# RWKV-7 and attention block on one core: another start of the chunk stage, and VectorE's last lane operations at another place in its steps

## The reference

```
def step(S, inp):
    r_t, w_t, k_t, v_t, a_t, b_t = inp
    sa = jnp.einsum('bhij,bhj->bhi', S, a_t)
    S = (S * w_t[:, :, None, :] + sa[..., None] * b_t[:, :, None, :]
         + v_t[..., None] * k_t[:, :, None, :])
    return S, jnp.einsum('bhij,bhj->bhi', S, r_t)
...
seq_in = tuple(u.transpose(1, 0, 2, 3) for u in (r_h, w_h, k_h, v_h, -kk, kk * a_h))
_, y = lax.scan(step, S0, seq_in)
```

## Time and profile before

| | us |
|---|---|
| median of three runs (1510.53 to 1513.07) | 1511.58 |
| the profiled execution's own time | 1514.68 |
| its span, first to last instruction | 1513.0 |
| PE busy in it | 1436.7 (95%) |
| DVE busy | 1033.1 (68%) |
| ACT busy | 739.6 (49%) |
| chunk stage: its first `l_products` to its last `quads` | 878.15 to 1060.35 |

### The profile page before, as it was taken

One profiled execution on the slowest core, in us unless ns is written; L12 is line 12 of the kernel. 1 busy time (PEld: TensorE's weight loads), 2 busy tenths in 40 slices (PEclk: granted clock), 3 DMA queues, 4 the chain that ended last, 5 costly groups with the idle time before them and its releaser, 6 DMA issues.

```text
span 1513.0 us, 30344 instructions
## 1 busy us (share of the span) xinstructions
PE 1436.7 (95%) x12931; PEld 1322.3 (87%) x12931; DVE 1033.1 (68%) x1463; ACT 739.6 (49%) x1071; POOL 93.5 (6%) x120
## 2 busy tenths in 40 slices
PE   6999999999999999998999967999799999999997
PEld 5898898999999999998999756889467898899986
DVE  5667577588844787577868665776678884488732
ACT  4555465445532455457588532433454553255422
POOL 3010011000030000000000231110000000000010
PEclk9999999999999999999999977999999999999999
DMA  4212221423433333555222232332333343334331
GB/s 126 67 57 63 64 70 50 113 84 98 123 92 100 92 92 88 158 162 173 83 74 77 70 85 47 60 57 40 113 84 98 98 123 104 95 85 112 86 96 56
DMA packets 283990, 136.78 MB, mean 90 GB/s; under 512 B 65449, under 2 KB 278593, under 8 KB 283601
## 3 DMA queue, kind: packets, MB, share of 16 engines
q1 hardware_dynamic: 283552, 134.77, 32.4%
q10 hardware_dynamic: 304, 0.08, 0.0%
HBM read 124.33 MB, written 10.49 MB: 89 GB/s over the span
## 4 chain that ended last, share of the span: by engine, by line
PE 74%; DVE 11%; ACT 6%; issue 3%; DMA 3%; POOL 1%; SPq 0%; DVEq 0%; POOLq 0%; ACTq 0%
PE psg L1882 25%; PE psx L1723 13%; PE psg L1723 11%; PE psg L2688 6%; PE psg L590 2%; DVE w_lo L136 2%; PE psx L590 2%; PE psg L618 2%; PE psg L674 1%; ACT rest_hi L330 1%; PE psx L3334 1%; DVE rest_lo L429 1%; DVE sum_lo L446 1%; ACT rest L316 1%; ACT w_hi L132 1%
## 5 line engine op out<-in xcount | busy, mean ns | idle before, releaser
L132 ACT ACTIVATE w_hi<-w_raw 128x1024 fp32r<-128x1024 f32 (+1 forms) x122 | 141.9, 1164 | 209.8 <-PE psg L1882 148.1
L1882 PE MATMUL psg<-mid_hi_l,w_hi 128*128 128x264 f32 (+1 forms) x720 | 232.8, 323 | 2.3 <-DVE w_lo L136 1.3
L1882 PE MATMUL psg<-mid_lo_l,w_hi 128*128 128x264 f32 (+1 forms) x720 | 231.6, 322 | 0.0
L1882 PE MATMUL psg<-mid_hi_l,w_lo 128*128 128x264 f32 (+1 forms) x720 | 231.0, 321 | 0.0
L136 DVE TENSOR_TENSOR w_lo<-w_raw,w_hi 128x1024 fp32r<-128x1024 f32 (+1 forms) x121 | 165.0, 1365 | 77.5 <-ACT w_hi L132 77.0
L1882 PEld LDWEIGHTS psg<-mid_hi_l,w_hi 128*128 128x128 f32 x720 | 135.3, 188 | 14.1 <-DVE w_lo L136 2.0
L1882 PEld LDWEIGHTS psg<-mid_lo_l,w_hi 128*128 128x128 f32 x720 | 135.3, 188 | 10.5 <-issue 0.2
L1882 PEld LDWEIGHTS psg<-mid_hi_l,w_lo 128*128 128x128 f32 x720 | 135.4, 188 | 10.3
L2688 PE MATMUL psg<-x_hi,w_hi 128*128 128x264 f32 (+1 forms) x320 | 99.7, 312 | 7.9 <-DVE w_lo L136 7.9
L2688 PE MATMUL psg<-x_lo,w_hi 128*128 128x264 f32 (+1 forms) x320 | 98.8, 309 | 0.0
L2688 PE MATMUL psg<-x_hi,w_lo 128*128 128x264 f32 (+1 forms) x320 | 98.7, 309 | 0.0
(11 more groups left out here) (518 smaller groups left out, 4336.1 us busy)
## 6 DMA issues: line engine op xcount, KB each, us to landing
w_raw<-in_w_ffn_out_dram SPq DMA_DIRECT2D x40, 704.0 KB, 4.7
w_raw<-in_w_qkv_dram SPq DMA_DIRECT2D x24, 512.0 KB, 3.7
w_raw<-in_w_rkv_dram SPq DMA_DIRECT2D x24, 512.0 KB, 3.9
x_raw_l<-in_w_ffn_in_dram SPq DMA_DIRECT2D x18, 512.0 KB, 4.1
x_raw_l<-in_w_ffn_in_dram SPq DMA_DIRECT2D x36, 256.0 KB, 4.7
w_raw<-in_w_ffn_in_dram SPq DMA_DIRECT2D x16, 512.0 KB, 3.8
y_raw_l<-in_w_ffn_in_dram SPq DMA_DIRECT2D x16, 512.0 KB, 4.0
y_raw_l<-in_w_ffn_in_dram SPq DMA_DIRECT2D x32, 256.0 KB, 4.5
```

The source lines that it names most:

```text
L132: k.nc.scalar.activation(k.w_hi[j][:, 0:kt, :], k.raw[j][:, 0:kt, :], ACT.Copy).then_inc(k.hi_ready[j].h, 1)
L1882: done = k.nc.tensor.matmul(self.bank(i, c), w[:, t, :], x, start=t == 0 and n == 0, stop=t == count - 1 and n == 2)
```

## The change

It replaces the loop's three short first steps by a start written out for each engine, and changes the steps themselves in three places.

- **Start.** The loop begins at c = 0. Ahead of it PE, ACT, DVE, POOL and SP have their own sequences for chunks 0 to 2, with `keep(8)`, `keep(44)`, `keep(36)` and, in step 0, another `keep(8)`. SP issues the first store of `low` ahead of the zero fills. `l_products(2)` now stands behind chunk 0's `a_v`, and DVE's `products(2)` behind `last_blocks(1)`; `l_products(3)`, `products(3)` and `small_blocks(2)` are in step 0.
- **Two buffers.** `lane_x`, `lane_xt` and the DRAM buffer of `low` are doubled, so that `small_blocks(n)` waits for the stores of chunk n - 2 and not of chunk n - 1.
- **Steps.** In steps 1 to 6 DVE's `last_blocks(c + 2)` moves from behind `next_t` to a place between the first and the second half of the masks. In every step that prepares, `turn_v` becomes eight transposes in place of eight matmuls with the identity. The halves of partitions for values and solve are swapped, as are the two planes of `bk`.

```diff
...
+    kept = lambda name: nc.dram_tensor(name, [H, (C // W) * LANE], F32).ap()
+    k.low_kept = [kept(f"low_kept{q}") for q in range(2)]
...
-            sp.wait_ge(zero_r.h, 4)
+            keep_low(0)
+            sp.wait_ge(zero_r.h, 1)
...
-            for c in range(-3, CHUNKS - 2):
-                if c + 3 < CHUNKS:
-                    keep_low(c + 3)
-                    fetch_lanes(c + 3)
-                if c == -3:
...
-                    sp.wait_ge(inv_in.h, 64)
-                else:
-                    keep_inverse(c + 2)
-                    fetch_inverse(c + 2)
+            fetch_lanes(0)
+            keep_low(1)
+            fetch_lanes(1)
+            sp.wait_ge(scaled_v.h, 1)
...
+            sp.wait_ge(inv_in.h, 64)
+            for n in range(CHUNKS):
+                if 1 < n < CHUNKS - 1:
+                    keep_low(n + 1)
+                    fetch_lanes(n + 1)
+                keep_inverse(n)
+                fetch_inverse(n)
+                if n == 1:
+                    keep_low(2)
+                    fetch_lanes(2)
...
             decays(1)
+            lower(0)
+            keys_turned(0, 0)
+            decays(2)
+            lower(1)
+            values_turned(0, 0)
+            end_decay(0, 0)
+            av_out(0, 0)
+            act.wait_ge(g_in.h, (1 + P // G_REST) * 16)
+            nc.scalar.activation(r.g_hi[:], r.g_raw[:], ACT.Copy).then_inc(g_split.h, 1)
+            lower(2)
+            decays(3)
             steps(act, step)
...
-                else:
-                    dve.wait_ge(inv_out.h, 32 * n)
+                elif n > 1:
+                    dve.wait_ge(inv_out.h, 32 * (n - 1))
...
-                if prep and n:
+                if prep:
                     next_t(n)
-                if 0 <= c + 2 < CHUNKS:
-                    last_blocks(c + 2)
-                if prep and n:
+                if c == 0:
                     next_xt(n, p, 0)
                     next_xs(n, p)
...
+                    small_blocks(2)
+                if c == 0 or not prep and c + 2 < CHUNKS:
+                    last_blocks(c + 2)
+                if prep and c:
+                    next_xt(n, p, 0)
+                    next_xs(n, p)
+                if prep and c:
+                    grow(q, c)
                 if prep:
                     keys(n, 0)
                     reads(n, p, 0)
+                    if 0 < c < CHUNKS - 2:
+                        last_blocks(c + 2)
                     keys(n, 1)
                     reads(n, p, 1)
...
             products(1)
-            dve.wait_ge(scaled_v.h, 2)
+            small_blocks(0)
+            last_blocks(0)
+            keys(0, 0)
+            keys(0, 1)
+            small_blocks(1)
+            last_blocks(1)
+            products(2)
             steps(dve, step)
...
-                    last = mm(pair_ps[C:P, m // 4, (m % 4) * P:(m % 4) * P + P], r.vv[:, m, n * C:n * C + C], k.ident[:],
-                              start=True, stop=True)
+                    last = nc.tensor.transpose(pair_ps[0:C, m // 4, (m % 4) * P:(m % 4) * P + P],
+                                               r.vv[:, m, n * C:n * C + C], k.ident[:])
...
             front_evicted(pe)
+            l_products(0)
+            turn_bk(0)
+            keep(8)
+            l_products(1)
+            turn_v(0)
+            quads(0, 0)
+            keep(44)
+            quads(0, 1)
+            a_v(0, 0)
+            keep(36)
+            l_products(2)
             steps(pe, step)
```

More of the change, by code:

```diff
@@ L111, in setup @@
     k.res_kept = nc.dram_tensor("res_kept", [P, KT, T], F32).ap()
[L112 to L113 removed]
+    kept = lambda name: nc.dram_tensor(name, [H, (C // W) * LANE], F32).ap()
+    k.low_kept = [kept(f"low_kept{q}") for q in range(2)]
+    k.inv_kept, k.turned_kept = kept("inverse_kept"), kept("inverse_turned_kept")
     return k
@@ L2967, in steps @@
         def steps(eng, step):
-            for c in range(-3, CHUNKS):
-                step(c, c + 1, c % 2, 0 <= c, 0 <= c + 1 < CHUNKS)
+            for c in range(CHUNKS):
+                step(c, c + 1, c % 2, c + 1 < CHUNKS)
         res_in, g_in, g_split, gate_d, gate_r = (
@@ L3046, in decays, with lower @@
                 if n > 1:
-                    nc.scalar.activation(bk[(n - 1) % 3][:, :, 1, :], chunk(r.kk_in, n - 1), ACT.Copy).then_inc(bk_r.h, 1)
+                    nc.scalar.activation(bk[(n - 1) % 3][:, :, 0, :], chunk(r.kk_in, n - 1), ACT.Copy).then_inc(bk_r.h, 1)
                 nc.scalar.activation(ch.w_ext[:, :, 1:C + 1], chunk(r.gs, n), ACT.Exp, scale=DECAY)
                 nc.scalar.activation(ch.w_inv[:], chunk(r.gs, n), ACT.Exp, scale=-DECAY).then_inc(exps.h, 1)
-            def step(c, n, q, chain, prep):
+            def lower(n):
+                act.wait_ge(lps.h, n + 1)
+                nc.scalar.activation(low[n % 3][:], l_ps, ACT.Copy).then_inc(low_r.h, 1)
@@ L3052, in step @@
+            def step(c, n, q, prep):
                 p = 1 - q
-                if c + 3 < CHUNKS:
-                    act.wait_ge(lps.h, c + 4)
-                    nc.scalar.activation(low[c % 3][:], l_ps, ACT.Copy).then_inc(low_r.h, 1)
+                if c + 3 < CHUNKS and c:
+                    lower(c + 3)
                 if prep:
[L3057 to L3060, removed]
@@ L3078, in step @@
                         act.wait_ge(state_r.h, c)
[L3079 to L3082, removed]
-                    nc.scalar.activation(r.g_hi[:], r.g_raw[:], ACT.Copy).then_inc(g_split.h, 1)
-                if chain and not prep:
+                    end_decay(n, p)
+                if not prep:
                     act.wait_ge(dx_d.h, level_count(c, 1))
@@ L3308, in l_products @@
                 for h, m, rows in heads:
-                    last = mm(l_ps[rows, m, :], r.xn[rows, m, n * C:n * C + C], bk[n % 3][rows, m, 0, :],
+                    last = mm(l_ps[rows, m, :], r.xn[rows, m, n * C:n * C + C], bk[n % 3][rows, m, 1, :],
                               start=True, stop=True)
@@ L3357, in a_v @@
                 for h, m, rows in heads:
-                    last = mm(a_ps[rows, m, :], akm[C:P, at(h), :], uv[p][C:P, at(h), :], start=True, stop=True)
+                    last = mm(a_ps[rows, m, :], akm[0:C, at(h), :], uv[p][0:C, at(h), :], start=True, stop=True)
                 last.then_inc(av_d.h, 1)
@@ L3420, in chain_u @@
                 for h, m, rows in heads:
-                    last = mm(u_ps[0:C, h % 2, m * C:m * C + C], xt[q][rows, m, :], wt[rows, m, :], start=True,
+                    last = mm(u_ps[C:P, h % 2, m * C:m * C + C], xt[q][rows, m, :], wt[rows, m, :], start=True,
                               stop=True)
@@ L3450, in gate, with step @@
                    skip_group_check=True).then_inc(gate_d.h, 1)
-            def step(c, n, q, chain, prep):
+            def step(c, n, q, prep):
                 p = 1 - q
-                if c + 3 < CHUNKS:
-                    l_products(c + 3)
-                if c < -1:
-                    keep(24)
-                if prep:
+                if c == 0:
                     turn_bk(n)
-                if c == 0:
                     turn_v(n)
@@ L3464, in step @@
                     quads(n, 0)
+                    l_products(3)
+                    keep(8)
                     times_x(n, p, 0)
```

190 lines of the change are left out of this document (102 added, 88 removed).

## The result

The changed kernel takes **1544.57 us** (median of 4 runs, 1541.02 to 1547.45) against 1511.58 for the kernel before (median of three): a ratio of **1.0218, 95% interval 1.0188 to 1.0248**, so it is slower. A fourth execution of the kernel before took 2803.71 us and is in neither the median nor the ratio. The forecast was 1542.7 in 1521 to 1560. Its profiled execution took 1547.45, with a span of 1545.7 against 1513.0: +32.7. X(1) comes at 944.91 instead of 946.20 (-1.29), the six intervals to X(7) last 135.97 instead of 103.05 (+32.92), and what is behind X(7) 464.82 instead of 463.75 (+1.07). The loss is all in the six intervals, as forecast. Inside them it is not put together as forecast.

A forecast was written before the change was run, and what follows sets the result against it. The prediction saw idle time in the start, little in the steps, and the moved last_blocks' DRAM round trip setting six intervals. Start -4.5, round trip +27.7, step 7 -0.9, clock +8.8: +31.1 on 1511.58, so 1542.7, range 1521 to 1560.

The forecast's parts named there:

- last_blocks moved, through DRAM: Steps 1 to 6: the inverse, born later, reaches the next times_x later; 21.8 us per interval, +27.7 in all.
- So it sets all six intervals: X(1) to X(7), each step's first times_x: the 21.8 us round trip exceeds 19.7 and 17.1, giving 130.8 in all.
- wrong if `times_x` starts without waiting for a transfer: Sign in the steps that would refute the forecast: times_x not held by the inverse's transfer.
- The masks: Steps 1 to 6: last_blocks delays the second mask by 2.6; full steps 19.7 us, steps 5 and 6 about 17.1.
- The clock: Steps 1 to 6: new TensorE gaps lower its clock, 2.2 in four of six steps; +8.8, between 0 and 32.
- falling after 3 us with 0.6 idle in them: Trace reading behind the clock term: TensorE's clock fell after 3 us that held 0.6 idle.
- The start: Ahead of X(1), step 1's first times_x: the new order brings it earlier; -4.5, the middle of 0.3 and 8.7.
- the two ends -0.3 and -8.7: Start: X(1) 0.3 earlier at mostly half clock, 8.7 earlier at full clock.
- The nearer of the two sums: Start, sum with half clock: quads at 935.7 and X(1) at 945.9, 0.3 earlier.
- turn_v: Steps 1 to 7: eight transposes for 16 matmul instructions take 0.87 us off the path.
- Behind X(7): Step 7, after its first times_x: no last_blocks, and the transposes save 0.87; -0.9.
- The interval of 19.7 by the 2.0 us of "DMA: Bandwidth & Descriptors": Round trip with the skill's 2.0 us transfer cost: interval 19.7 instead of 21.8, six costing 15.1 instead of 27.7.

The follow-up runs named there:

- e1: Changed kernel with last_blocks put back ahead of the subtractions in steps 1 to 6, all else as changed: 1502.76 us, ratio 0.9940.
- e2: Changed kernel whose fetches from the third chunk on read the second chunk's stored inverse, so no round trip: 1528.10 us, ratio 1.0109.
- e11: e1 with SyncE's store of the inverse held until the step's second mask: 1543.38 us, ratio 1.0220.
- e8: e2 with 20 unused matmuls where TensorE waits for the second mask: 1520.33 us, ratio 1.0069.
- e4: Changed kernel with 20 unused matmuls where TensorE waits for the second mask, round trip kept: 1546.45 us, ratio 1.0229.
- e10: Changed kernel with last_blocks back in front in steps 1 to 4, behind the first masks in 5 and 6: 1518.35 us, ratio 1.0044.
- e6: e1 with SyncE's store of the inverse held until the copy of a_v: 1557.62 us, ratio 1.0295.
- e9: Changed kernel with last_blocks back in front in steps 5 and 6 only: 1524.68 us, ratio 1.0087.
- e5: e1 with turn_v's eight transposes written as matmuls with the identity: 1511.09 us, ratio 0.9981.
- e3: Changed kernel with GpSimd's products held until the first masks are done, round trip kept: 1546.95 us, ratio 1.0219.

## Why the prediction was right, and where it wasn't

Two bounds could set a step, and each was run alone, at the clock that it left TensorE. Sums of intervals in us:

| | four full steps | last two |
|---|---|---|
| before | 71.77 | 31.28 |
| e1, neither | 67.31 | 29.20 |
| chain through the mask alone (e2) | 88.24 | 33.82 |
| round trip alone (e11) | 89.88 | 46.41 |
| both (the changed kernel) | 90.11 | 45.86 |

- **last_blocks moved, through DRAM: right in mechanism, 0.9 small.** Forecast 21.8 an interval; e11 shows 22.7 in the mean, and 21.70 in its one interval at full clock. The forecast had 12.6 from X to the store and 9.2 from there to X. The second is right (9.19 in the mean of the three X's that waited). The first is 12.8 in step 5, 13.2 to 13.4 in the full steps, where the lane product takes 1.92 to 1.95 beside GpSimd, and 15.1 in step 6, where TensorE runs at half clock behind its wait.
- **"So it sets all six intervals": this step failed.** By the prediction's own sign ("wrong if `times_x` starts without waiting for a transfer") three of six X's speak against it. It does set the last two, by 12.0 us (45.86 against 33.82). In the full steps the chain alone is as long as the round trip, and taking either one away gives back at most 1.9 of 90.11.
- **The masks: a full step forecast at 19.7 came to 22.06 (e2).** Missing were 1.0 for the overlap of the lane product with GpSimd (4.98 less 3.96) and 1.80 for the clock (e8 against e2); less these it is 19.2. The forecast had also kept the 0.3 that VectorE's own product lost beside GpSimd before (1.01 for 0.69) and loses no more; with it, it is 19.6. The last two were forecast at 17.1, and took 16.91.
- **The clock: +8.8 was put on top of the round trip.** What the six intervals cost over 130.8 is 5.2. The lapse comes behind the wait for the mask, not mainly before `times_x`. That wait was forecast at 1.3, with TensorE given 2.96 + 1.1 of work behind the first mask; in step 4 it has 2.98, and waits 3.35. Removing the lapse there moves nothing (e4), because the round trip bounds it too. It shows where the chain alone sets the step: 1.80 in each of four. The prediction's "falling after 3 us with 0.6 idle in them" leaves out that TensorE was busy only 0.10 of the 3 us in which the clock fell; e8 held 1.00 with 2 us idle in 6.
- **The start: -4.5 forecast, -1.29 measured**, inside the two ends -0.3 and -8.7. X(0) comes 6.1 earlier (921.15; 927.24 before), but from there to X(1) it takes 23.76 at a granted clock of 0.53:

```profile
921.00:944.91 23.91, 15.96 (x280) 14.06 (x281) 14.20 (x40) 3.52 (x7) 2.50 (x2) 0.53 0.26 45
```

  The nearer of the two sums was that at half clock: the last `quads` came at 934.01, forecast 935.7. In ten of the eleven other runs X(1) lies between 939.8 and 944.8, in e10 at 946.43, though several edits lie behind it. Up to X(1) seven programs agree (e1, e4, e6, e9, e10, e11 and the changed kernel); their traces have it at 940.54 to 946.43, 943.4 in the mean, 2.8 earlier than the one trace before. So the 1.29 is one execution's, in a spread of 5.9, and does not refute the 4.5. What spreads it was not tried.
- **turn_v: -0.87 forecast, -0.90 measured** (e5 against e1).
- **Behind X(7): -0.9 forecast, +1.07 measured.** e1, where X(7) waits for nothing, has -2.46 there. In the 19 us behind X(7) the granted clock is 1.00 in e1 and 0.84 in the changed kernel. The forecast had no lapse behind the last wait.
- **The interval of 19.7 by the 2.0 us of "DMA: Bandwidth & Descriptors" in the Trainium skill** is given without its sum. With 2.0 in place of 3.2 the forecast's terms give 20.6 if only the last landing changes, and 19.4 if the one before the first fetch does too.

So errors met: the start gained 3.2 less than forecast, the six intervals lost 3.6 less (32.92 for 36.5), and the part behind X(7) lost 2.0 more (+1.07 for -0.9). The total of +31.1 came out as +32.7. The direction and the size of the round trip were understood; that the total is within 2 us is luck.

In the trace GpSimd and VectorE slow each other when the lane product, which reads two tensors in SBUF, runs beside GpSimd's. The masks, which read one input in PSUM, took 0.69 beside GpSimd's first product before, and that one 1.29 (993.34 above). The Trainium skill, "GPSIMD Engine Reference", section "Key points", says this: contention comes with VectorE instructions that have two SBUF inputs or run in a 2-port mode. The trace agrees (1.92 against 1.17). It gives no figure, but it would have pointed at the missing 1.0 in the masks' chain.

## What to carry to other kernels

When a long operation is moved behind a producer, work out both chains that cross it, the one of the engine's next consumers and the one of its own result: here both came to 22 to 23 us in the full steps, and removing one alone gave little; in the last two only the round trip did. An order is tested best by a table of each bound alone, neither, and both. Before moving work on VectorE, look at what GpSimd does at the new place, not only at what VectorE waits for.

## What was not expected of the hardware

- A 64x512 VectorE product of two SBUF tensors takes 1.08 (before) to 1.17 alone and 1.92 beside GpSimd's 128x512 product, which takes 2.12 instead of 1.29; a 64x256 copy takes 0.62 instead of 0.37. GpSimd's first product kept its time, and each operation that overlapped the one before it on the other engine ended 0.95 (lane product), 0.55 (VectorE's 128x512 product, e3) or 1.12 to 1.13 (GpSimd's second) behind its end. That they wait for one another is an inference from these times; no run tests it.
- Eight f32 turns with the identity are 8 instructions in 1.06 us as transposes and 16 in 1.96 as matmuls.
- With TensorE's wait for the mask filled by 2.56 us of unused matmuls, its granted clock stayed at 1.00 through a step with 2 us of idle time left (e8).
